# A hybrid decoder step: eight KB of SBUF handed from stage to stage, weights split a step sooner, and a selection step parted in two

## The chip, the cores and the metric

One core of one Trainium2 chip. The metric is the time of one execution on the device, in microseconds. The median of three runs of the kernel before is 2760.28 us (2756.52, 2760.28, 2761.57). The engines: TensorE (PE; its weight loads are written PEld), VectorE (DVE), ScalarE (ACT), GpSimd (POOL), and SyncE (SP), whose queue issues nearly all the DMAs.

## What is computed

One inference step of two layers, for a prompt of 1024 tokens and 8 samples of 8 new tokens each. Layer 0 is attention, layer 1 a recurrent block, and a squared-ReLU MLP follows each. Everything is fp32. The change is all in layer 0 and its hand-over to what follows:

```python
def attn_projections(xn, w_in, a_q_norm, a_k_norm, b_q_norm, b_k_norm):
    h = jnp.einsum('btd,de->bte', xn, w_in)             # one product: 1024 -> 3656 columns
    qa, ka, va, qi, ki, wi, hb = jnp.split(h, list(SPLIT_POINTS), axis=-1)
    q_a = rmsnorm(qa.reshape(bsz, t, A_HEADS, HEAD_DIM), a_q_norm)     # by heads of 64
    ...
    q_b = rmsnorm(hb[:, :, :, 0], b_q_norm[:, None, :])

# prompt, block by block of 128 queries
sc = index_scores(qi_blk, wi_blk, ki)                   # then causal mask
_, idx = lax.top_k(sc, topk)                            # 256 keys of each query
o_a = sparse_attend(q_a, k_a[idx], v_a[idx], ...)       # 8 heads, 2 kv heads
for g, (win, dil) in enumerate(((128, 1), (512, 4), (2048, 16))):
    o, l = dilated_attend(q_b[g], k_b[g], v_b[g], ...)  # local attention, 4 heads
o_b = merge_groups(outs, lses)
y = jnp.einsum('bte,ed->btd', jnp.concatenate([o_a, o_b], axis=-1), w_out)
```

The samples do the same against caches. x + y goes on to the MLP.

## The kernel before

**Stages.** The program is a row of stages, each a block in which every engine has its own list of instructions; between blocks all engines meet at a barrier. In layer 0: `stage_project` (0 to 464 us of PE's time), `stage_window` (local attention, to 574), `stage_sparse` (577 to 729), `stage_sample` (to 776), `stage_out_projection` (from 779). SBUF tensors of a stage are allocated when it is entered, so nothing of the next stage can be loaded before its barrier, except for what `SparseKeys`, `Samples` and `OwnRows` hold.

**fp32 as two halves.** Each fp32 product is three matmul passes: high x high, low x high, high x low. A weight unit of 128 rows is loaded by SP (`load_w`, into `w_raw`, three slots), cast to its high half by DVE (`split_high`, line 881), and its low half, raw minus high, is made by POOL (`split_unit_low`, line 570).

**Projection.** The columns of w_in are taken in eight groups (line 56): kikv (0), qi (1), qa (2), three of qk (3 to 5), v01 (6), v2 (7, half as wide). A group has 9 tiles of up to 128 rows (the first is the 64 sample rows), a tile is 8 units x 3 passes = 24 matmuls into one of three PSUM banks (line 738). PE waits for all eight low halves of a group at its first tile, and for the copy of the tile three before. ACT copies each tile out (line 674), scaled by the row's norm; then for q and k heads the squares (ACT, line 694), sums by head and mean (DVE, lines 912 and 917), root (ACT, line 627), inverse and product (DVE, lines 924 and 928), the gain (POOL, line 596), and the store to DRAM by SP (line 515). The norm is in two parts, `norm_sum` of a tile and `norm_apply` of the one before it. From group 2 on, a step is one (group, tile), and in each of the first eight steps of a group DVE and POOL also split one unit of the next group.

**Selection.** The 256 largest scores of a query are found by bisection on the bits of a bound. For two of the six score tiles DVE itself counts (`Select.count_at`, line 238; a count over 384 and one over 512 scores) and moves the bound (lines 254 and 256: flip, bound), in `Select.step`, once per step. For the four others ACT sums signs (`show`, line 277) and DVE turns their bound (`turn`, lines 288 to 297: count, flip, minus_bound). The main loop of DVE, per step (group, tile):

```python
split_high(gi + 1, i)
if n and STEPS[n - 1] in SHOW_AT: sel.turn(dve, SHOW_AT[STEPS[n - 1]])
norm_sum(gi, i)
norm_apply(*before)
sel.step(dve, y)          # two counts, flip, bound
```

POOL's, per step: `split_unit_low`, then the gains of the tile (two of 256 columns in the qk groups, one of 512 in qa).

**Local attention** runs 24 jobs, each 128 rows of one group: SP loads q, k, v rows (line 1424, 384 KB, eight slots, six ahead) and the bias of each group (line 1429); SP's list begins with row load 0, bias 0, row load 1. PE turns q and k (line 1496), ACT copies them, PE makes scores (1507), DVE adds the bias and finds the maximum (1562), ACT takes the exponent, PE turns the probabilities (1520), PE multiplies by the values (1531), DVE packs (1569), SP stores (1448). PE's list is one job apart per part: turn_rows(t), scores(t-1), turn_probs(t-2), outputs(t-3).

**Sparse attention** begins with turn_keys(0), turn_keys(1) (line 1221), turn_queries(0) (1230), each copied out of the same PSUM bank by ACT (1163), and then scores (1243). SP loads queries of two blocks first (1097).

**Out projection.** SP's list: weight units 0 and 1 (2267), the core's own attention rows a and b (1589, 1596), params, x in four parts (2108, 2111), units 2 and on (2117), two slots. DVE: high half of unit 0, low half of the first mixed rows (`low_of(0)`, line 2341), high half of unit 1, its low half (2358), low_of(1) and on. POOL makes the low half of unit 0 and of units 2 and on (2128). PE: line 2156 for the first two units, 2141 for the others.

## Time and profile before

| | us |
|---|---|
| median of 3 runs | 2760.28 |
| lowest, highest | 2756.52, 2761.57 |
| the profiled execution, its time | 2755.16 |
| its span (first to last instruction) | 2753.3 |
| mean granted TensorE clock, share of full speed | 0.978 |

In layer 0 PE stands still for more than 3 us at eight places:

| PE idle, us | at | before |
|---|---|---|
| 8.93 | 0 | first tile of group 0 |
| 4.56 | 46.8 | group 1 |
| 9.92 | 222.2 | group 3 |
| 6.84 | 463.9 | local attention |
| 3.64 | 573.8 | sparse attention |
| 4.17 | 729.3 | sample stage |
| 12.80 | 776.0 | out projection |
| 3.56 | 811.4 | third weight unit of the out projection |

How to read a row in order of time: start in us from the span's start, duration in us, engine (SPq is the queue of SP), line of the kernel, operation, output<-inputs, how many are taken together, and in brackets the engine's idle time just before with what ended it. PEclk is the granted clock as a share of 2.4 GHz. Matmuls are pipelined, and their ends are modelled; spans on POOL are rough.

### The profile page before, as it was taken

The page shows a single profiled execution, that of the slowest core. Times are in us where ns is not written, and L with a number is a line of the kernel's source. Part 1 is how long each engine was busy: PE and PEld are TensorE (multiplying, and loading weights), DVE is VectorE, ACT ScalarE, POOL GpSimd, SP SyncE. Part 2 cuts the span into 40 slices and gives each one's busy share as a digit, 9 for nine tenths or more (in the row PEclk, how much of TensorE's full clock was granted, in tenths as well). Part 3 has the DMA queues.
Part 4 walks back from the last instruction along what each step waited for, and adds up shares of the span by engine and source line. Part 5 has one row for each costly group of instructions (what it writes and reads, how often), then busy time and mean ns, then how long its engine had stood idle before and what let it go on. Part 6 is the DMA issues. An engine that isn't in the chain of part 4 may idle for free.

```text
span 2753.3 us, 39744 instructions
## 1 busy us (share of the span) xinstructions
PE 2639.0 (96%) x15960; PEld 2450.4 (89%) x15960; DVE 1134.3 (41%) x1978; ACT 779.7 (28%) x1400; POOL 952.7 (35%) x471
## 2 busy tenths in 40 slices
PE   8998998978879999999999999998999999999999
PEld 6666777856659999999999999998999999999999
DVE  5468875335455322222222256655432222222222
ACT  5357773865422110011001033443211001000100
POOL 4214440026335342343334263233344233323422
PEclk8999998989889999999999999999999999999999
DMA  4402223623551111111111112132111111111112
GB/s 147 134 18 83 86 85 104 193 75 109 163 201 47 53 40 46 46 38 46 46 45 39 46 31 86 66 140 111 41 46 47 39 44 46 46 38 46 46 39 87
DMA packets 109196, 198.65 MB, mean 72 GB/s; under 512 B 22709, under 2 KB 62773, under 8 KB 108805
## 3 DMA queue, kind: packets, MB, share of 16 engines
q1 hardware_dynamic: 104602, 191.85, 21.9%
q10 hardware_dynamic: 4480, 5.27, 0.5%
q8 instruction: 72, 1.18, 0.2%
q14 instruction: 42, 0.34, 0.0%
HBM read 170.97 MB, written 47.17 MB: 79 GB/s over the span
## 4 chain that ended last, share of the span: by engine, by line
PE 64%; issue 3%; POOL 2%; DVE 1%; ACT 1%; SPq 1%; DMA 0%; POOLq 0%; DVEq 0%; ACTq 0%
PE d_ps L2141 62%; POOL m_hidden_low L2470 2%; PE d_ps L2763 1%; ACT m_relu L2494 1%; POOL unit_low L2128 1%; DMA unit_raw<-w_units 0%; DVE unit_high L2124 0%; DVE xg_low L2891 0%; SPq L1596 0%; PE d_ps_sums L2199 0%; SPq L1589 0%; DVE r_tanh L2875 0%; SPq L2111 0%; POOLq L2416 0%; DVE r_input_gate L2869 0%
## 5 line engine op out<-in xcount | busy, mean ns | idle before, releaser
L2128 POOL TENSOR_TENSOR unit_low<-unit_raw,unit_high 128x1024 fp32r<-128x1024 f32 x159 | 449.1, 2825 | 1200.8 <-DVE unit_high L2124 1194.8
L2141 PE MATMUL d_ps<-xg_high,unit_high 128*128 128x364 f32 (+1 forms) x2112 | 471.9, 332 | 5.7 <-DVE xg_low L2891 3.1
L2141 PE MATMUL d_ps<-xg_low,unit_high 128*128 128x364 f32 (+1 forms) x2112 | 464.8, 328 | 0.0
L2141 PE MATMUL d_ps<-xg_high,unit_low 128*128 128x364 f32 (+1 forms) x2112 | 464.6, 328 | 0.0
L2494 ACT ACTIVATE m_relu<-d_ps 128x1092 f32<-128x1092 f32 x64 | 69.3, 1083 | 1178.0 <-PE d_ps L2141 1178.0
L2557 DVE TENSOR_TENSOR x_t<-x_t,d_ps 128x1092 f32<-128x1092 f32 x128 | 165.3, 1291 | 520.3 <-PE d_ps L2141 520.3
L2141 PEld LDWEIGHTS d_ps<-xg_high,unit_high 128*128 128x128 f32 x2112 | 365.7, 188 | 11.4 <-DVE xg_low L2891 4.2
L2141 PEld LDWEIGHTS d_ps<-xg_high,unit_low 128*128 128x128 f32 x2112 | 366.6, 188 | 0.0
L2141 PEld LDWEIGHTS d_ps<-xg_low,unit_high 128*128 128x128 f32 x2112 | 365.6, 188 | 0.0
L2141 PE MATMUL d_ps<-m_hidden_high,unit_high 128*128 128x364 f32 (+1 forms) x1536 | 340.7, 330 | 4.0 <-POOL m_hidden_low L2470 4.0
L2141 PE MATMUL d_ps<-m_hidden_high,unit_low 128*128 128x364 f32 (+1 forms) x1536 | 338.5, 328 | 0.0
L2141 PE MATMUL d_ps<-m_hidden_low,unit_high 128*128 128x364 f32 (+1 forms) x1536 | 337.9, 328 | 0.0
L2544 DVE TENSOR_TENSOR m_relu<-m_relu,rstd_all 128x1092 f32<-128x1092 f32 x64 | 86.4, 1350 | 562.3 <-ACT m_relu L2494 562.3
L2141 PEld LDWEIGHTS d_ps<-m_hidden_high,unit_high 128*128 128x128 f32 x1536 | 264.0, 188 | 12.0 <-POOL m_hidden_low L2470 8.8
L2141 PEld LDWEIGHTS d_ps<-m_hidden_high,unit_low 128*128 128x128 f32 x1536 | 266.0, 188 | 0.0
L2141 PEld LDWEIGHTS d_ps<-m_hidden_low,unit_high 128*128 128x128 f32 x1536 | 265.7, 188 | 0.0
L738 PE MATMUL proj_ps<-w_high,x_high 128*128 128x512 f32 (+2 forms) x520 | 202.7, 390 | 16.6 <-POOL w_low L570 16.6
L738 PE MATMUL proj_ps<-w_low,x_high 128*128 128x512 f32 (+2 forms) x520 | 198.9, 382 | 0.0
L738 PE MATMUL proj_ps<-w_high,x_low 128*128 128x512 f32 (+2 forms) x520 | 198.4, 382 | 0.0
L2470 POOL TENSOR_TENSOR m_hidden_low<-m_square,m_hidden_high 128x1092 fp32r<-128x1092 f32 x64 | 164.0, 2562 | 6.4 <-DVE m_square L2549 6.4
L738 PEld LDWEIGHTS proj_ps<-w_high,x_high 128*128 128x128 f32 x520 | 100.0, 192 | 50.0 <-POOL w_low L570 18.6
L2124 DVE CAST unit_high<-unit_raw 128x1024 fp32r<-128x1024 f32 x158 | 112.4, 712 | 59.7 <-PE d_ps L2141 58.7
(354 smaller groups left out, 3084.6 us busy)
## 6 DMA issues: line engine op xcount, KB each, us to landing
unit_raw<-w_units SPq DMA_DIRECT2D x160, 512.0 KB, 3.5
w_raw<-w_in SPq DMA_DIRECT2D x48, 256.0 KB, 2.9
proj_rows<-rows SPq DMA_DIRECT2D x32, 256.0 KB, 2.0
s_win<-win_cache SPq DMA_DIRECT2D x2, 3968.0 KB
sw_rows<-proj_rows SPq DMA_DIRECT2D x16, 384.0 KB, 4.8
proj_rows<-rows SPq DMA_DIRECT2D x36, 128.0 KB, 1.8
select_work<-xt SPq DMA_DIRECT2D x8, 546.0 KB, 3.7
x_t<-xt SPq DMA_DIRECT2D x4, 1092.0 KB, 9.5
```

The costliest lines, as they stand in the source:

```text
L738: last = nc.tensor.matmul(ps[p % 3][:, 0:w], x[:, k, c:c + P], y[gi % 2][:, k, 0:w], start=(n == 0), stop=(n == len(passes) - 1))
L2124: self.nc.vector.tensor_copy(self.wh[slot][:, :], self.raw[:, slot, :]).then_inc(self.w_high, 1)
L2128: self.nc.gpsimd.tensor_tensor(self.wl[slot][:, :], self.raw[:, slot, :], self.wh[slot][:, :].bitcast(F32), ALU.subtract).then_inc(self.w_ ...
L2141: last = self.nc.tensor.matmul(ps[:, c, 0:USED[c]], w[wslot][:, wk], v[:, k, c, 0:USED[c]], start=(k == 0 and n == 0), stop=(k == nk - 1 a ...
L2470: nc.gpsimd.tensor_tensor(hl[:, i, :, :], v[:, i % 2, :, :], hh[:, i, :, :].bitcast(F32), ALU.subtract).then_inc(h_low, 1)
L2494: nc.scalar.activation(r[:, i % 2, :, :], ps[slot][:, :, 0:CH], ACT.Relu).then_inc(d.taken[slot], 1)
L2544: nc.vector.tensor_tensor(r[:, i % 2, :, :], r[:, i % 2, :, :], d.rstd[:, :, :], ALU.mult).then_inc(relu_scaled, 1)
L2557: nc.vector.tensor_tensor(d.x[:, n, :, :], d.x[:, n, :, :], ps[s][:, :, 0:CH], ALU.add).then_inc(d.taken[s], 1)
L2763: last = nc.tensor.matmul(ps[use % 2][:, c, 0:CC], gw[:, n % 2, x, :], cv[:, n % 2, c, :], start=True, stop=True)
```

## The change

1. **A class `Handover`** holds 8 KB of each SBUF partition, allocated from the start of the program to its end, and semaphores that go with it. It is used in turn as the raw weights and gains of the projections, the first two row slots and one turned slot of local attention, the queries of sparse attention, one tensor of new values of the samples, and the raw weight units of the dense stages.
2. **Projection, weights.** Units 0 to 2 of group 3 are loaded, and split by POOL, at the last step of group 1, and cast by DVE among and after the scores; units 3 to 7 go at steps 0 to 4. Of groups 4 and on, each unit is loaded and split one step sooner: unit k at step k - 1 of the group before, and unit 0 at the last step of the group two before (there behind the norms on DVE, behind the gains on POOL).
3. **Projection, DVE's list.** `Select.step` is parted in `try_own` (the two counts), now before `norm_sum`, and `move_own` (flip, bound), after `norm_apply`.
4. **Local attention.** At tile 4 of the last group SP waits for all low halves and for the stores of three tiles, and loads the first two row blocks ahead of the barrier. In the stage bias 0 is loaded first.
5. **Sparse attention.** Both halves of the keys, and the queries of block 0, are turned in the last iterations of local attention (PE, ACT); SP loads two blocks of queries there after store 20. The stage then begins with scores.
6. **Out projection.** Units 0 and 1 and the own rows but those of group 2 are loaded at the end of the sample stage, after waits for the stores of those rows. SP's list in the out projection becomes: own rows of group 2, params, unit 2, x part 0, unit 3, x parts 1 to 3, unit 4 and on. DVE makes both high halves and the second low half, and only then low_of(0).

```diff
+class Handover:
+
+
+    def __init__(self, nc, ctx):
+        self.all = ctx.enter_context(nc.sbuf_tensor("unit_raw", [P, 2, KD * P], F32))
+        self.flat = self.all[:, :, :].rearrange("p u n -> p (u n)")
+        self.rows = self.flat[:, 0:2 * 3 * BW].rearrange("p (s n) -> p s n", s=2)
+        self.rows_in = [ctx.enter_context(nc.semaphore(f"sw_first_in{i}")) for i in range(2)]
+        self.unit_in = [ctx.enter_context(nc.semaphore(f"d_w_in{i}")) for i in range(2)]
...
-        dve.wait_ge(self.done, self.n)
-
-    def step(self, dve, y):
+
+    def try_own(self, dve, y):
+
+        bound = self.bound[:, :].bitcast(F32)
+        self.count_at(dve, range(OWN_TILES), lambda x: bound[:, x:x + 1] if y else 0.0)
+
+    def move_own(self, dve, y):
 
         nc = self.nc
         part = slice(0, OWN_TILES)
-        bound = self.bound[:, :].bitcast(F32)
-        self.count_at(dve, range(OWN_TILES), lambda x: bound[:, x:x + 1] if y else 0.0)
+        dve.wait_ge(self.done, self.n)
         said = self.count[:, part].bitcast(I32)
         if y == 0:
             self.mark(nc.vector.tensor_scalar(self.bound[:, part], said, 31, 1 << 30, ALU.arith_shift_right, ALU.bitwise_xor))
...
-        wraw = sb("w_raw", [P, NRAW, 512])
+        wraw = hand.flat[:, 0:512 * NRAW].rearrange("p (s n) -> p s n", s=NRAW)
...
+        AHEAD_3 = 3
+        WEIGHTS_AT = {n: [] for n in range(len(STEPS))}
+        for k in range(AHEAD_3, KD):
+            WEIGHTS_AT[k - AHEAD_3].append((3, k))
+        for gi in range(4, NGR):
+            for k in range(KD):
+                WEIGHTS_AT[NT * (gi - 3) + k - 1].append((gi, k))
...
-                if gi + 1 < NGR and k < KD:
+                if gi < 2 and k < KD:
                     load_w(gi + 1, k)
+                if gi == 1 and i == NT - 1:
+                    for k in range(AHEAD_3):
+                        load_w(3, k)
+                if gi >= 2:
+                    for unit in WEIGHTS_AT[NT * (gi - 2) + i]:
+                        load_w(*unit)
...
+                if (gi, i) == (NGR - 1, 4):
+                    sp.wait_ge(S["w_low"], KD * NGR)
+                    for n in range(rows_n(gi, 0), rows_n(gi, 3)):
+                        sp.wait_ge(stored[n % NST], stored_total(n))
+                    for t in range(2):
+                        c = TS + P * t
+                        sp.dma_start(hand.rows[:, t, :], proj[c:c + P, 768:768 + 3 * BW]).then_inc(hand.rows_in[t], 16)
...
-                    if gi + 1 < NGR and k < KD:
+                    if gi < 2 and k < KD:
                         split_unit_low(pool, gi + 1, k)
+                    if gi == 1 and i == NT - 1:
+                        for k in range(AHEAD_3):
+                            split_unit_low(pool, 3, k)
+                    if gi >= 2 and i < NT - 1:
+                        for unit in WEIGHTS_AT[NT * (gi - 2) + i]:
+                            split_unit_low(pool, *unit)
                     for h0, hn, row, _ in kinds(gi):
                         n = rows_n(gi, i)
                         pool.wait_ge(S["normed"], NORM_AT[gi, i] + 1)
                         v = st[:, n % NST, HD * h0:HD * (h0 + hn)].rearrange("p (h d) -> p h d", h=hn)
                         nc.gpsimd.tensor_tensor(v, v, gains[:, row:row + 1, :].broadcast_to([P, hn, HD]),
                                                 ALU.mult).then_inc(S["gained"], 1)
+                if gi >= 2:
+                    for unit in WEIGHTS_AT[NT * (gi - 2) + NT - 1]:
+                        split_unit_low(pool, *unit)
                 if gi == 1:
...
+                if j == 6:
+                    split_high(3, 0)
+            for k in range(1, AHEAD_3):
+                split_high(3, k)
...
-            parts = [(sel.step, y) for y in range(BITS + 1)] + [(sel.close, x, z) for x in range(OWN_TILES) for z in range(sel.SLICES)]
+            parts = [("own", y) for y in range(BITS + 1)] + [("close", x, z) for x in range(OWN_TILES) for z in range(sel.SLICES)]
...
-                if gi + 1 < NGR and i < KD:
-                    split_high(gi + 1, i)
+                if i < NT - 1:
+                    for unit in WEIGHTS_AT[n]:
+                        split_high(*unit)
                 if n and STEPS[n - 1] in SHOW_AT:
                     sel.turn(dve, SHOW_AT[STEPS[n - 1]])
+                r1 = min(len(parts), len(parts) * (n + 1) // (last + 1))
+                own = [at[0] for what, *at in parts[r0:r1] if what == "own"]
+                if own:
+                    sel.try_own(dve, own[0])
                 if kinds(gi):
                     norm_sum(gi, i)
                     if before:
@@ -1000,9 +1056,17 @@
                 elif before:
                     norm_apply(*before)
                     before = None
-                r1 = min(len(parts), len(parts) * (n + 1) // (last + 1))
+                if i == NT - 1:
+                    for unit in WEIGHTS_AT[n]:
+                        split_high(*unit)
+                if own:
+                    sel.move_own(dve, own[0])
+                for y in own[1:]:
+                    sel.try_own(dve, y)
+                    sel.move_own(dve, y)
                 for what, *at in parts[r0:r1]:
-                    what(dve, *at)
+                    if what == "close":
+                        sel.close(dve, *at)
...
+    def load_q(self, sp, proj, j):
+        dst = self.q[:, j % 2, :].rearrange("p (r g d) -> p g r d", r=REP, g=AG)
+        for g in range(AG):
+            sp.dma_start(dst[:, g], proj[TS + P * j:TS + P * (j + 1), 256 * g:256 * (g + 1)].rearrange(
+                "p (r d) -> p r d", r=REP)).then_inc(self.q_in[j % 2], 16)
...
-            for n in range(3):
-                take_turn(n)
...
-            turn_keys(0)
-            turn_keys(1)
-            turn_queries(0)
             scores(0)
...
-            load(0)
             load_bias(0)
-            for t in range(1, AHEAD):
+            for t in range(2, AHEAD):
                 load(t)
...
+                if t == NJ - 4:
+                    for j in range(2):
+                        keys.load_q(sp, proj, j)
...
+                if t >= NJ:
+                    take_key_turn(t - NJ, keys.kt[:, 512 * (t - NJ):512 * (t - NJ + 1)])
+            take_key_turn(2, keys.qt[:, 0, :])
...
+            def turn_keys(n):
+                if n == 0:
+                    pe.wait_ge(keys.all_in, 16 * keys.LOADS)
+                    pe.wait_ge(turn_taken, NJ)
+                else:
+                    pe.wait_ge(keys.turn_taken, n)
+                if n == 2:
+                    pe.wait_ge(keys.q_in[0], 16 * AG)
+                for i in range(4):
+                    v = keys.kr[:, 4 * n + i, :] if n < 2 else keys.q[:, 0, P * i:P * (i + 1)]
+                    last = nc.tensor.transpose(psx[:, P * i:P * (i + 1)], v, ident[:, :])
+                last.then_inc(keys.turned, 1)
...
+                if t == NJ + 2:
+                    turn_keys(2)
                 if t >= 3:
                     outputs(t - 3)
+                if NJ <= t < NJ + 2:
+                    turn_keys(t - NJ)
...
+            for x in range(NA):
+                sp.wait_ge(o_out[x % NO], 16 * (x // NO + 1))
+            own.load_a(sp)
+            sp.wait_ge(pv_done, NA + 4)
+            for u in range(2):
+                sp.dma_start(hand.all[:, u, :], a["w_units"][u]).then_inc(hand.unit_in[u], 16)
+            for n, g in enumerate((1, 0)):
+                for x in range(NA + DB // 4 * n, NA + DB // 4 * (n + 1)):
+                    sp.wait_ge(o_out[x % NO], 16 * (x // NO + 1))
+                own.load_b(sp, g)
...
         @block.sync
         def _(sp):
-            for u in range(2):
-                sp.dma_start(d.raw[:, u, :], a["w_units"][u]).then_inc(d.w_in[u], 16)
-            own.load_a(sp)
-            for g in range(NG):
-                own.load_b(sp, g)
-            d.load_first(sp)
-            for u in range(2, KD + 2):
+            own.load_b(sp, 2)
+            d.load_params(sp)
+            for i in range(2):
+                d.load(sp, 2 + i, i)
+                d.load_x(sp, i)
+            for i in range(2, XPARTS):
+                d.load_x(sp, i)
+            for u in range(4, KD + 2):
                 d.load(sp, u, u % 2)
...
             weights_high(0)
-            low_of(0)
             weights_high(1)
             dve.wait_ge(d.w_high, 2)
             nc.vector.tensor_tensor(d.wl[1][:, :], d.raw[:, 1, :], d.wh[1][:, :].bitcast(F32), ALU.subtract).then_inc(second_low, 1)
-            for k in range(1, NK):
+            for k in range(NK):
                 low_of(k)
```

## Rows read from the trace of the kernel before

**Rows 1.** The page, first part: busy time, share of the span, instructions.

```profile
PE 2639.0 (96%) x15960; PEld 2450.4 (89%) x15960; DVE 1134.3 (41%) x1978; ACT 779.7 (28%) x1400; POOL 952.7 (35%) x471
```

**Rows 2.** The waits of PE: us in total, how many times, the longest.

```profile
PE proj_ps L738 <- POOL w_low L570: 16.6, 5, 9.9
...
PE sw_ps_x L1496 <- DMA sw_rows<-proj_rows: 8.6, 2, 6.8
```

**Rows 3.** Busy time by stretches, from four stages; columns in the first row.

```profile
core 0: us, PE busy (x) PEld busy (x) DVE busy (x) ACT busy (x) POOL busy (x), PEclk, DMA share, GB/s
285.96:336.50 50.54, 50.36 (x216) 40.48 (x216) 43.54 (x125) 40.83 (x82) 22.71 (x26) 1.00 0.28 84
438.08:463.93 25.85, 25.85 (x217) 25.65 (x215) 24.80 (x37) 4.50 (x9) 0.00 (x0) 1.00 0.15 49
463.93:483.40 19.47, 9.78 (x56) 7.87 (x57) 3.70 (x18) 7.91 (x24) 0.31 (x1) 0.56 0.67 233
568.70:596.00 27.30, 19.26 (x85) 13.10 (x85) 5.64 (x31) 9.90 (x37) 4.70 (x4) 0.50 0.19 44
```

**Rows 4.** In order of time, around group 3: start, us, engine, line, operation.

```profile
232.15 0.79 PE L738 MATMUL proj_ps<-w_high,x_high 128*128 128x512 f32 x1 [9.92 <-POOL w_low L570]
...
214.59 1.29 POOL L570 TENSOR_TENSOR w_low<-w_raw,w_high 128x512 fp32r<-128x512 f32 x1
...
230.82 1.27 POOL L570 TENSOR_TENSOR w_low<-w_raw,w_high 128x512 fp32r<-128x512 f32 x1
...
232.08 0.67 ACT L674 ACTIVATE rows<-proj_ps,rstd_rows 128x512 f32<-128x512 f32 x1
```

**Rows 5.** In order of time, one step of group 4: DVE, then POOL.

```profile
248.77 0.69 DVE L928 TENSOR_TENSOR rows<-rows,head_inverse 128x512 f32<-128x512 f32 x1
...
251.05 1.22 DVE L256 SCALAR_TENSOR_TENSOR select_bound<-select_flip,select_bound 128x2 int32<-128x2 int32 x1
...
249.54 1.45 POOL L596 TENSOR_TENSOR rows<-rows,gain_rows 128x256 f32<-128x256 f32 x2 [3.15 <-DVE rows L928]
250.94 1.31 POOL L570 TENSOR_TENSOR w_low<-w_raw,w_high 128x512 fp32r<-128x512 f32 x1
```

**Rows 6.** Groups by line, DVE, 286 to 387 us (busy, mean ns).

```profile
L238 DVE TENSOR_SCALAR_CACHE_REDUCE late<-select_work,select_bound 128x384 f32<-128x384 f32 (+1 forms) x34 | 23.0, 676 | 0.6
L256 DVE SCALAR_TENSOR_TENSOR select_bound<-select_flip,select_bound 128x2 int32<-128x2 int32 x17 | 18.5, 1088 | 0.6
...
L912 DVE TENSOR_REDUCE head_sums<-rows_sq 128x8 f32<-128x512 f32 x18 | 12.3, 686 | 11.2 <-ACT rows_sq L694 11.2
...
L297 DVE SCALAR_TENSOR_TENSOR select_minus_bound<-select_flip,select_minus_bound 128x4 int32<-128x4 int32 x13 | 2.1, 163 | 0.4
```

**Rows 7.** In order of time, start of local attention: SP, PE, DVE.

```profile
467.49 0.33 SPq L1424 DMA_DIRECT2D sw_rows<-proj_rows  x1
...
470.77 1.11 PE L1496 MATMUL sw_ps_x<-ident,sw_rows 128*128 128x128 f32 x4 [6.84 <-DMA sw_rows<-proj_rows]
...
476.04 0.29 DVE L1562 CUSTOM_DVE_ANT_0 sw_scores<-sw_ps_s,sw_bias 128x128 f32<-128x128 f32 x1 [10.78 <-PE sw_ps_s L1507]
```

**Rows 8.** In order of time, PE, start of sparse attention.

```profile
577.41 1.09 PE L1221 MATMUL sa_ps_x<-ident,sa_keys 128*128 128x128 f32 x4 [3.64 <-PEq L1369]
...
582.86 1.23 PE L1243 MATMUL sa_ps_s<-sa_keys_t,sa_queries_t 64*128 64x128 f32 x8 [0.69 <-ACT sa_queries_t L1163]
```

**Rows 9.** In order of time, out projection: SP, DVE, PE, DVE, POOL, PE.

```profile
779.04 0.35 SPq L2267 DMA_DIRECT2D unit_raw<-w_units  x1
...
785.73 2.93 DVE L2341 TENSOR_TENSOR mixed_low<-mixed_low,mixed_high 128x1024 fp32r<-128x1024 f32 x1 [0.58 <-ACT mixed_high L2295]
...
788.76 0.94 PE L2156 MATMUL d_ps<-mixed_high,unit_high 128*128 128x364 f32 x2 [12.80 <-DVE mixed_low L2341]
...
810.72 0.69 DVE L2124 CAST unit_high<-unit_raw 128x1024 fp32r<-128x1024 f32 x1 [0.91 <-DMA unit_raw<-w_units]
...
811.49 3.40 POOL L2128 TENSOR_TENSOR unit_low<-unit_raw,unit_high 128x1024 fp32r<-128x1024 f32 x1 [10.40 <-DVE unit_high L2124]
...
814.94 1.27 PE L2141 MATMUL d_ps<-mixed_high,unit_high 128*128 128x364 f32 x3 [3.56 <-POOL unit_low L2128]
```

113 lines of the change are left out of this document (55 added, 58 removed).

## The prediction

> **What bounds the kernel now.** I read four views, in this order. The page: TensorE (PE) is busy for 96% of the span [rows 1], so apart from doing fewer or quicker matmuls, which this change does not attempt, time can only come out of PE's idle stretches and out of stretches where its clock is down. The list of waits, PE first: it names what PE stood still for; the two largest that the change touches are the split weights in the projection stage (16.6 us in five waits, one of 9.9) and the first rows of local attention (8.6 us) [rows 2]. The busy time by stretches: the granted clock is 0.56 after the hand-over from the projections to local attention and 0.50 around the one to sparse attention (1.2 GHz against 2.4 elsewhere) [rows 3], so each hand-over is paid twice, once idle and once slow. Last, the instructions in order of time at each of these places. The dense stages after 830 us wait for little and are not touched.
>
> The profiled execution took 2755.16 us; the median of the runs shown is 2760.28, 5.1 more. I sum against the former and carry the difference over to the median. A measurement of this kernel can tell about 0.2% (5.5 us) from no change.
>
> **Part 1, weights split one step sooner (lines 570, 881).** PE idles 9.92 us before group 3, because the last low half of its weights, unit 7, is made on GpSimd (POOL) at 230.82 and done at 232.09 [rows 4]. With three units split ahead, unit 7 takes the place of unit 4, which POOL began at 214.59 [rows 4], 15 us sooner; PE leaves group 2 at 222.2, so this wait goes whole. The other groups win one step of about 5.6 us, more than any of their waits; of the 16.6 us some 12 can go: the 9.9, and 2 of the other four waits' 6.7, most of which stand before group 1, which is left as it is. The two tiles' worth of slow clock behind the gap can go as well: the first matmul after it takes 0.79 us [rows 4] where the stretch at full clock has 216 in 50.54 us, 5.6 us a tile of 24 [rows 3]; I put this at 2.8 us. If PE alone decided, part 1 would give 12 + 2.8, less a little, **-14.5 us**. The three early casts of VectorE (DVE) lie in waits for the scores, three splits of POOL too; POOL's six mask selects wait behind the latter, but no count reads them before group 2. The loads of SyncE (SP) move with them, one step earlier, and do not pass a store that anyone is late for.
>
> But PE may be only three tiles ahead of the copies by ScalarE (ACT), as it has three banks. ACT copies tile (2,8) at 232.08, 9.9 us after PE made it, since between copies it does the sign passes of the selection (line 277), each of which needs the bound that DVE turned after the last. So once PE waits for no weights, the chain ACT-DVE-POOL decides, and part 2 changes that chain.
>
> **Part 2, DVE's counts ahead of the norms (lines 228 to 256).** Today a step is: cast, turn, head sums, norm, two counts, flip, bound. At 248.77 the norm runs to 249.46; its end releases two gain products on POOL (249.54, 1.45 us together) and the next split (250.94, 1.31) [rows 5]. The counts run beside the gains unhindered. The flip and the bound do not: the bound, two words a lane, takes 1.22 us and ends 0.02 after POOL's split [rows 5]; its mean over 17 is 1088 ns, where the turn's same operation on four words takes 163 [rows 6], mostly while POOL is idle. So DVE and POOL exclude each other for such operations, whoever started first finishing, and one that follows by a semaphore loses to a POOL instruction that is already waiting. The Trainium skill has this as a rule (SBUF — State Buffer, Who interferes with whom): casts, tensor_scalars and anything with two SBUF inputs on VectorE need the port pair shared with GpSimd, for the whole instruction, while a tensor_scalar with an accumulator does not. This trace agrees (1.22 us and unhindered counts), and the rule speaks against the new order.
>
> New order: cast, turn, counts, head sums, norm, flip, bound. Now nothing that is free of the conflict follows the norm. From the norm's end: flip 0.1; bound behind the first gain, 0.85; cast 1.2 and the turn's first operation 1.35; its second behind the second gain, 2.1; its third behind the split, 3.3; then counts 1.45 (two at 676 ns mean and their readouts [rows 6]), head sums to norm 1.7: 6.5 us. A step without a turn: 1.2 + 1.45 + 1.7 = 4.4. Three steps of four have one: mean 6.0 us, against 5.57 to 5.6 of PE. Before, DVE waited 11.2 us in 18 steps for ACT [rows 6], so it needed 5.6 - 0.6 = 5.0. Hence the chain becomes the bound: copies of group 2 come up to 2.5 us later; (3,0) is copied at 236.5 instead of behind PE, (6,0) at 236.5 + 27 x 6.0 = 398.5. There PE may be ahead by between 0 and 9.9 us; I take 4, and then 9 tiles of 5.57 and 9 of 2.87 (nine in 25.85 us [rows 3]), where no gains are left, less the one already made: 398.5 - 4 - 5.6 + 75.9 = 464.8. PE ends this stage at 463.93 now [rows 3]. **Parts 1 and 2 together: +0.9 us.** Bounds: -14.5 where the conflict costs nothing; +9 at 6.3 us a step, if each blocked operation waits 10% longer.
>
> **Part 3, first rows handed over (line 1424).** SP's first instruction of local attention is at 467.49 (row load, 3.3 us to PE's first transpose at 470.77), the first scores are read at 476.04 [rows 7]. With rows 0 and 1 already there, PE starts at 467.5, and two transposes, two copies and the scores need 4.2 us as now: 471.7. The bias, now first in the queue, should need little more than that row load, and lands about then. Saved 4.3; row 2 comes some 0.4 late. **-3.9**, bounds -2 (bias lands last) and -5. SP's wait for three stores at tile (7,4) holds one store back a little, where ACT is busy 4.5 of 25.85 us [rows 3] and can be late; free.
>
> **Part 4, keys and first queries turned before the barrier (lines 1221, 1230).** The first scores of sparse attention start at 582.86; its first transposes began at 577.41 [rows 8]: 5.45 us of turns and copies. They move into the tail of local attention. Two fit into idle spots; the last (turn_keys(2)) waits for ACT's second key copy and stands ahead of the last outputs: up to 2.2 us at the low clock (twice a batch of 1.09 [rows 8]), nothing if it fits in beside them. I take 1.6: **-3.9**, bounds -2.5 and -6. Four query loads on SP stand before the stores of jobs 21 to 23; only the last of these stores holds the barrier, and it has three jobs to make that up. Next to be late is ACT's exponent, as now.
>
> **Part 5, units and own rows loaded in the sample stage (lines 2267, 1589, 1596).** PE waits 12.80 us, to 788.76, for the first low half of the mixed rows: that subtraction took 2.93 us from 785.73 [rows 9] behind POOL's split. The stage starts at 779.0 [rows 9]. With both units there by then the splits run while the mixed rows come in: POOL's done by 782.9, DVE's own low half by 784.1, then the first low half 1.2 us: 785.3, **-3.5**. Unit 2 no longer queues behind the 4.4 MB of x. Its cast, 0.91 us late at 810.72, follows the x addition at once, and POOL's 3.40 us at 811.49 shrink to 2.4 as it starts first [rows 9]: **-1.9** of the 3.56 us idle at 814.94. The matmuls after that gap start slow (three in 1.27 us [rows 9]); I count half of an estimated 1.4 us: **-0.7**. Together -6.1, bounds -2 (mixed rows land no sooner) and -8.5. Own loads sit behind work that is done; the barrier waits for the last stores as before.
>
> **Sum.** +0.9 - 3.9 - 3.9 - 6.1 = **-13.0 us**: 2742.2 for such an execution, **2747.3** as a median.
>
> **Rivals.** (a) *The conflict does not decide*: DVE's short operations slip in ahead of POOL, or ACT's slack swallows them. Then part 1 keeps its gain, -14.5 - 13.9 = -28.4: 2731.9. For it: ACT itself is busy for 40.83 us in nine tiles [rows 3], 4.5 a tile, and could catch up. Against: 17 bounds at 1088 ns [rows 6]. Chance 0.27. (b) *The chain at 6.3 us a step*: +9 - 13.9 = -5, 2755; the same as now. 0.13. (c) *Slower*: each blocked operation waits for two POOL instructions, not one: another 0.9 us a step, 6.9, over 36 steps +33 - 13.9 = +19: 2779. It decides from about 6.5 us a step on (36 x 0.93 = 33 over PE's pace, less the 14.5 of part 1, against 13.9 elsewhere, plus 5.5). Against: every blocked bound ends with one instruction. 0.05. (d) *The hand-overs give half*, since the barriers stay: -6. In the forecast's range. Forecast: 0.55, 2740 to 2754.
>
> The range runs from (a) to (b), 2730 to 2757. Faster by over 0.2% (below 2754.8): the forecast but for a tenth, and (a): 0.79. Slower: (c) and a little: 0.06. Same: 0.15.
>
> **What would show it.** Part 1: no idle before group 3, PE's waits there turn from POOL's w_low to ACT's copies. Part 2: the bound's mean falls below 1 us, but the turn's operations (lines 288 to 297) rise above 0.17 us each, and copies in groups 3 to 5 are 6.0 us apart; at 5.57 rival (a) is right. Part 3: PE's first transpose with SP's first load. Part 4: scores first in the sparse stage. Part 5: PE idle of 9 to 10 us before the out projection. The number fails if the step is not near 6.0, for each 0.1 us is 3 to 4 us.

## The result, and the profile after

The changed kernel takes 2738.06 us (median of 4 runs, 2733.07 to 2744.03) against 2759.95 for the one before: a ratio of 0.9925, 95% interval 0.9908 to 0.9942, so 16 to 25 us are gone. The forecast was 2747.3. The profiled execution took 2744.03 us, its span 2742.2: the longest among its runs, which matters below.

TensorE's landmarks in the two profiled executions (us from the start), and what each stretch between them gained:

| TensorE | before | changed | gained in the stretch | forecast |
|---|---|---|---|---|
| last product of the projections | 463.93 | 465.11 | -1.2 | -0.9 |
| first score of sparse attention | 582.86 | 574.29 | 9.8 | 7.8 |
| last product of sparse attention | 729.29 | 724.13 | -3.4 | 0 |
| last product of the sample stage | 775.96 | 771.46 | -0.7 | 0 |
| first product of the out projection | 788.76 | 783.55 | 0.7 | 3.5 |
| first product of weight unit 2 | 814.94 | 806.75 | 3.0 | 1.9 |
| end of the span | 2753.3 | 2742.2 | 2.9 | 0.7 |

The page of the changed kernel (busy us, share, instructions), the line that answers to [rows 1], and the two longest entries of its list of waits of PE, which answer to [rows 2]:

```profile
PE 2642.6 (96%) x15960; PEld 2452.6 (89%) x15960; DVE 1149.1 (42%) x1978; ACT 781.2 (28%) x1400; POOL 953.9 (35%) x471
```

```profile
PE d_ps L2254 <- DVE mixed_low L2440: 12.1, 1, 12.1
PE proj_ps L785 <- POOL w_low L608: 11.6, 2, 5.9
```

The wait of 9.9 us before group 3 is gone, but the weights still cost 11.6 us in two waits: one before group 1 (5.9, from 47.18 to 53.12) and a new one of 5.65 before group 4. The row of the first product behind it:

```profile
286.17 0.79 PE L785 MATMUL proj_ps<-w_high,x_high 128*128 128x512 f32 x1 [5.65 <-POOL w_low L608]
```

Groups of DVE by line over the same stretch as [rows 6] (L250 is the count, L271 the bound, L303 and L310 the first two operations of the turn; line, operation, count, then busy us and mean ns, then idle before):

```profile
L250 DVE TENSOR_SCALAR_CACHE_REDUCE late<-select_work,select_bound 128x384 f32<-128x384 f32 (+1 forms) x36 | 24.3, 676 | 0.7
...
L271 DVE SCALAR_TENSOR_TENSOR select_bound<-select_flip,select_bound 128x2 int32<-128x2 int32 x17 | 12.1, 712 | 0.6
L310 DVE TENSOR_SCALAR select_flip<-select_count 128x4 int32<-128x4 int32 x14 | 10.8, 768 | 0.5
...
L303 DVE TENSOR_TENSOR select_count<-select_signs,select_level 128x4 f32<-128x4 f32 x14 | 5.4, 387 | 4.0 <-ACT late L292 3.7
```

The bound fell from 1088 to 712 ns, and the turn's operations rose: the second takes 768 ns, the first 387, where (in e1, below) 170 and 235 are to be had. Both are as the list of what to look for said. The third sign of that list, ScalarE's copies 6.0 us apart in groups 3 to 5, or 5.57 if rival (a) is right, came out in between: the nine from (3,0) at 240.51 to (4,0) at 294.72 are 6.02 apart, the 18 from there to (6,0) at 396.33 are 5.65 apart.

One step in order of time, DVE and then POOL (start, us), shows why the turn's operations take longer:

```profile
261.60 0.72 DVE L271 SCALAR_TENSOR_TENSOR select_bound<-select_flip,select_bound 128x2 int32<-128x2 int32 x1
262.24 0.41 DVE L928 CAST w_high<-unit_raw 128x512 fp32r<-128x512 f32 x1
262.95 0.32 DVE L303 TENSOR_TENSOR select_count<-select_signs,select_level 128x4 f32<-128x4 f32 x1 [0.30 <-ACT late L292]
263.31 1.21 DVE L310 TENSOR_SCALAR select_flip<-select_count 128x4 int32<-128x4 int32 x1
...
261.56 1.69 POOL L640 TENSOR_TENSOR rows<-rows,unit_raw 128x256 f32<-128x256 f32 x2 [3.33 <-DVE rows L975]
263.22 1.28 POOL L608 TENSOR_TENSOR w_low<-unit_raw,w_high 128x512 fp32r<-128x512 f32 x1
```

The norm (not shown) releases POOL's two gains at 261.56. The bound, the cast and the turn's first operation squeeze in between and behind them; POOL's split begins at 263.22, and the turn's second operation, begun at 263.31, ends at 264.52, 0.02 after the split (263.22 + 1.28 = 264.50). That is the picture of [rows 5] again, with another victim.

The granted clock by stretches (us, busy us of PE, PEld, DVE, ACT, POOL, then PEclk, DMA share, GB/s), answering to [rows 3]:

```profile
core 0: us, PE busy (x) PEld busy (x) DVE busy (x) ACT busy (x) POOL busy (x), PEclk, DMA share, GB/s
174.00:182.00 8.00, 7.79 (x45) 5.90 (x45) 3.24 (x4) 3.75 (x7) 3.84 (x8) 0.84 0.16 39
182.00:190.00 8.00, 8.00 (x30) 5.61 (x29) 0.89 (x3) 3.39 (x7) 0.24 (x1) 0.50 0.09 29
286.00:387.00 101.00, 100.83 (x423) 81.54 (x424) 93.17 (x253) 81.34 (x162) 48.83 (x53) 0.97 0.29 89
585.00:600.00 15.00, 13.42 (x85) 8.29 (x83) 6.46 (x26) 8.84 (x33) 1.56 (x1) 0.75 0.37 88
```

From 179.4 us, during the small products of the sample scores, the clock stands at 0.50, though TensorE was busy for 7.79 of 8 us; and it was down for two stretches of 3.4 us in sparse attention, where the kernel before had none behind its first scores' slow stretch. Both are in the table above as losses, as the 2.9 us won behind 806.75, where TensorE's list is the same, go with fewer such stretches (one of 3.4 us, against three before; one of those three is the slow start behind 814.94 that the forecast counted at 0.7). Whether they belong to the change is taken up in e0. From 286 to 387 TensorE is busy for 100.83 of 101 us.

Local attention and the first scores of sparse attention, answering to [rows 7] and [rows 8] (PE, DVE, PE):

```profile
468.39 0.63 PE L1578 MATMUL sw_ps_x<-ident,unit_raw 128*128 128x128 f32 x4 [3.29 <-PEq L371]
...
472.41 0.29 DVE L1648 CUSTOM_DVE_ANT_0 sw_scores<-sw_ps_s,sw_bias 128x128 f32<-128x128 f32 x1 [5.97 <-DMA sw_bias<-window_strips]
...
574.29 1.23 PE L1298 MATMUL sa_ps_s<-sa_keys_t,unit_raw 64*128 64x128 f32 x8 [3.64 <-PEq L1421]
```

And the out projection, answering to [rows 9] (SP's load of two weight units, an ACT copy that waits for a store, the first instruction of the stage on POOL, the first product, the first product of unit 2):

```profile
766.21 0.83 SPq L1858 DMA_DIRECT2D unit_raw<-w_units  x2
...
774.13 0.38 ACT L1950 ACTIVATE ss_merged_t<-ss_ps_x 128x256 f32<-128x256 f32 x1 [4.18 <-DMA mixed_t<-ss_merged_t]
...
777.64 0.15 POOL L2376 MEMSET ones_square<- 128x64 f32 x1 [7.71 <-POOLq L1771]
...
783.55 0.94 PE L2254 MATMUL d_ps<-mixed_high,unit_high 128*128 128x364 f32 x2 [12.10 <-DVE mixed_low L2440]
...
806.75 0.76 PE L2239 MATMUL d_ps<-mixed_high,unit_high 128*128 128x364 f32 x3 [1.53 <-POOL unit_low L2226]
```

### The profile page after: what moved, and what is told of

Its sections match the earlier page's. It is cut to its first block, busy times and chain, and to the rows that moved or that the text cites. A ratio compares the mean times of both kernels' runs of the same rounds, so it can differ in the third digit from the quotient of the medians.

```text
span 2742.2 us, 39751 instructions
## 1 busy us (share of the span) xinstructions
PE 2642.6 (96%) x15960; PEld 2452.6 (89%) x15960; DVE 1149.1 (42%) x1978; ACT 781.2 (28%) x1400; POOL 953.9 (35%) x471
## 4 chain that ended last, share of the span: by engine, by line
PE 64%; issue 3%; POOL 2%; DVE 1%; ACT 1%; POOLq 0%; DVEq 0%; ACTq 0%
PE d_ps L2239 63%; POOL m_hidden_low L2568 2%; PE d_ps L2861 1%; ACT m_relu L2592 1%; PE d_ps L2254 1%; POOL unit_low L2226 1%; DVE unit_high L2222 0%; DVE xg_low L2989 0%; PE d_ps_sums L2297 0%; DVE unit_low L2456 0%; DVE r_tanh L2973 0%; POOLq L2514 0%; DVE r_input_gate L2967 0%; DVE r_tanh L2961 0%; DVE x_t L2655 0%
## 5 line engine op out<-in xcount | busy, mean ns | idle before, releaser
L2239 PEld LDWEIGHTS d_ps<-m_hidden_low,unit_high 128*128 128x128 f32 x1536 | 265.7, 188 | 0.0
L785 PE MATMUL proj_ps<-w_high,x_high 128*128 128x512 f32 (+2 forms) x520 | 203.1, 391 | 11.7 <-POOL w_low L608 11.6
L785 PEld LDWEIGHTS proj_ps<-w_high,x_high 128*128 128x128 f32 x520 | 100.3, 193 | 44.1 <-POOL w_low L608 12.3
```

Source lines behind the costliest of these rows:

```text
L785: last = nc.tensor.matmul(ps[p % 3][:, 0:w], x[:, k, c:c + P], y[gi % 2][:, k, 0:w], start=(n == 0), stop=(n == len(passes) - 1))
L2239: last = self.nc.tensor.matmul(ps[:, c, 0:USED[c]], w[wslot][:, wk], v[:, k, c, 0:USED[c]], start=(k == 0 and n == 0), stop=(k == nk - 1 a ...
```

## Experiments

Each kernel is the changed one with the edit shown. "Ratio" is to the kernel before, run in the same session. Where stretches of the profile are compared, a half-clock stretch is named if it is in one and not in the other.

### e0: the changed kernel again

> The changed kernel once more, as it is, to see which of its stretches repeat. The profile after shows the clock at half from 179.4 to 193.1 us and from 592.4 and 636.8 us, at places where the kernel before had it whole. Theory A: these are chance of one execution; then a second profile has its half-clock stretches elsewhere, PE ends the projections some 5 to 7 us sooner (458 to 460 instead of 465.1), and the span is near 2732 to 2736. Theory B: they come with the change (the weight splits moved in front of the sample scores); then they stand at the same places again and PE ends the projections at 465 again. In both the median is 0.991 to 0.994 of the kernel before.

Measured: 2737.25 us, ratio 0.9925 (0.9909 to 0.9942). Its profiled execution has nearly the same slow stretches (13.7 us from 178.4, 3.4 from 591.4 and from 635.8) and the same wait of 5.67 us before group 4; the projections end at 464.42. By this run alone theory B (they come with the change) stood. The later runs with the very same projection code took that away: executions of f1, f2 and g1 have no half-clock stretch at 179 and end the projections at 459.52, 459.52 and 458.99, that of g2 has it and ends at 463.99. The same two rows, of the kernel f2 (keys back, projection unchanged):

```profile
174.00:182.00 8.00, 7.81 (x61) 6.23 (x60) 3.24 (x4) 3.49 (x8) 4.08 (x8) 1.00 0.26 65
182.00:190.00 8.00, 8.00 (x37) 5.95 (x36) 6.00 (x20) 2.80 (x5) 0.00 (x0) 1.00 0.01 4
```

So of six executions of this projection three had the slow stretch, and they end the stage 4.5 to 6.1 us later. The stretch itself costs 4.1 to 4.7 of that: from the start of GpSimd's 21st split to that of its 28th (162.97 to 199.41 in the changed kernel) it takes 36.1 to 36.7 us with it and 32.0 without; the rest was there before. In the four executions with the counts behind the norms (the kernel before, e1, e3, h1) the stretch did not occur; that is too few to say whether it is chance. The two short ones in sparse attention come and go likewise: with none of them that stage takes 146.4 to 146.6 us (before, e1, f1, h1), with one 147.8 (e2, h3), with two 149.7 to 149.8 (the changed kernel, e0, e3, g1); in f2, g2 and h2 the slow stretch at the stage's start was itself longer. The 3.4 us that the table shows as given back are these. What decides whether an execution has them was not found; up to 179 us the six kernels ran the same instructions.

### e1: counts behind the norms again (part 2 undone)

```diff
-                if own:
-                    sel.try_own(dve, own[0])
                 if kinds(gi):
...
                 if own:
+                    sel.try_own(dve, own[0])
                     sel.move_own(dve, own[0])
```

> The changed kernel with part 2 alone undone: the two counts stand again behind norm_apply, right before flip and bound; weights stay a step sooner, hand-overs stay. Theory (the port that VectorE and GpSimd share decides): the counts behind the norm cover the gains, VectorE's step falls from 5.74 us (turn steps 6.26, others 4.2) to below TensorE's 5.57, the 5.65 us wait for the weights of group 4 is gone, and TensorE ends the projections 8 to 14 us sooner than in the changed kernel, at 451 to 457; the bound's mean goes back to about 1.1 us. Ratio to the kernel before some 0.987 to 0.990. Rival (the order is not what decides; the wait at group 4 comes from the late start of the steps): TensorE's end moves by less than 2 us. Second rival (the new order was worth something, since ScalarE's root gets its sums at once): it ends later than 467.

Measured: 2732.37 us, ratio 0.9910 (0.9892 to 0.9927). The first product of group 4, and the same groups of DVE over the same stretch:

```profile
275.62 0.51 PE L785 MATMUL proj_ps<-w_high,x_high 128*128 128x512 f32 x1 [2.25 <-POOL w_low L608]
...
L271 DVE SCALAR_TENSOR_TENSOR select_bound<-select_flip,select_bound 128x2 int32<-128x2 int32 x16 | 16.2, 1014 | 0.5
...
L303 DVE TENSOR_TENSOR select_count<-select_signs,select_level 128x4 f32<-128x4 f32 x14 | 3.3, 235 | 2.9 <-ACT late L292 2.8
...
L310 DVE TENSOR_SCALAR select_flip<-select_count 128x4 int32<-128x4 int32 x14 | 2.4, 170 | 0.5
```

The projections end at 453.43, without a slow stretch at 179; against the 459.0 to 459.5 of the executions of the changed projection that had none either, the new order costs 5.6 to 6.1 us. Counted from GpSimd's 28th split, behind the slow stretch, it is 5.7 to 6.2: 265.2 to 265.7 us to the end of the stage in the six executions of the changed projection, 259.5 in e1 and in h1, which has the same order as e1. Both are below the 8 to 14 expected, since nearly half of the distance to 465.11 was the clock. The wait before group 4 is 2.25 instead of 5.65, not gone. The turn's operations are back at 235 and 170 ns, the bound at 1014. The rivals (no change, or later than 467) are out. By times the two kernels are 4.9 us apart, and the intervals of the ratios overlap, though each of the five runs of e1 (2728.73 to 2735.81) is shorter than each of the five of e0 (2736.23 to 2746.56).

### e2: weights at the old steps (part 1 undone)

```diff
-        AHEAD_3 = 3
+        AHEAD_3 = 0
...
-                WEIGHTS_AT[NT * (gi - 3) + k - 1].append((gi, k))
+                WEIGHTS_AT[NT * (gi - 3) + k].append((gi, k))
...
-                if j == 6:
-                    split_high(3, 0)
-            for k in range(1, AHEAD_3):
-                split_high(3, k)
```

> The changed kernel with part 1 alone undone: every weight unit is loaded and split at the step of the kernel before, counts stay ahead of the norms. Theory (shared port): now the slower chain of VectorE also makes the weights late; a wait of about 10 us before group 3 is back, there are more before groups 4 to 6, and TensorE ends the projections at 475 to 480, 10 to 15 us later than in the changed kernel. Ratio to the kernel before about 1.000. Rival (the order costs nothing): only the 9.9 us and the slow clock behind it come back and the end is at 464 plus 1 to 5, that of the kernel before plus little.

Measured: 2756.09 us, ratio 0.9990 (0.9978 to 1.0002); the projections end at 481.14 (with the slow stretch at 179). All that the hand-overs win is lost again. Its waits of PE for weights:

```profile
PE proj_ps L785 <- POOL w_low L608: 24.7, 5, 11.6
```

One before each of the groups 1 and 3 to 6 (11.64, 2.89, 1.80 and 2.45 us for the latter). In e3, with the same weight steps and the old order, they are 16.8 us in five waits: with weights just in time, the slower steps of DVE go into them.

### e3: both at once (hand-overs alone)

The two edits above together.

> The changed kernel with parts 1 and 2 undone, so the hand-overs between stages alone are left (parts 3, 4 and 5). TensorE ends the projections at 464 as in the kernel before (within 1.5 us); what is won comes behind it. Theory (my sum for these parts): 13.9 us, 0.995 of the kernel before. Rival (half of it is given back behind the gaps, as the profile after hints for sparse attention, where 3.4 us of 8.6 are lost again by 724 us): 7 to 10 us, 0.9965.

Measured: 2744.68 us, ratio 0.9947 (0.9928 to 0.9966); the projections end at 464.64, as before. The hand-overs are worth 14.9 us by medians, where the forecast's sum for them was 13.9. The four kernels make a square, medians in us:

| | counts behind the norms | counts ahead |
|---|---|---|
| weights at the old steps | 2744.7 | 2756.1 |
| weights one step sooner | 2732.4 | 2737.3 |

Part 1 alone is worth 12.3, part 2 alone costs 11.4; on top of part 1 it costs 4.9. TensorE's waits for weights show the same: the new order adds 7.9 us to them at the old weight steps (16.8 to 24.7) and 2.9 with weights a step sooner (8.7 to 11.6), where the weights' lead swallows the rest.

### h2: GpSimd's gains made small

```diff
-                        v = st[:, n % NST, HD * h0:HD * (h0 + hn)].rearrange("p (h d) -> p h d", h=hn)
-                        nc.gpsimd.tensor_tensor(v, v, gains[:, row:row + 1, :].broadcast_to([P, hn, HD]),
+                        v = st[:, n % NST, HD * h0:HD * (h0 + hn)].rearrange("p (h d) -> p h d", h=hn)[:, :, 0:1]
+                        nc.gpsimd.tensor_tensor(v, v, gains[:, row:row + 1, 0:1].broadcast_to([P, hn, 1]),
```

> The changed kernel, with the gain products of GpSimd cut to one column in 64 of each head (so 63 of 64 columns of queries and keys go without their gain); their number and all waits stay. It takes 1.3 to 1.45 us of GpSimd's work out of each step. Theory (VectorE's short operations behind the norm wait for GpSimd's gains and split): the turn's first and second operations fall from 460 and 776 ns to below 250, VectorE's step falls below TensorE's 5.57, and TensorE ends the projections at 446 to 454 (459.5 in executions of the changed projection without the half-clock stretch at 179 us, 465 with it). Rival (it is the order itself, ScalarE being asked for its root and squares later): 458 or later.

Measured: 2727.51 us, ratio 0.9884 (0.9865 to 0.9904); the projections end at 449.05, no wait before group 4. The bound and the turn's second operation:

```profile
L271 DVE SCALAR_TENSOR_TENSOR select_bound<-select_flip,select_bound 128x2 int32<-128x2 int32 x15 | 2.6, 172 | 0.5
...
L310 DVE TENSOR_SCALAR select_flip<-select_count 128x4 int32<-128x4 int32 x13 | 2.2, 170 | 0.4
```

Not an instruction of DVE was touched, and the bound went from 712 to 172 ns, the turn's second operation from 768 to 170. So what held them was GpSimd's work, not the order of ScalarE's requests. The order matters by what it leaves under that work.

### h3: flip and bound ahead of the norm as well

```diff
                 if own:
                     sel.try_own(dve, own[0])
+                    sel.move_own(dve, own[0])
...
-                if own:
-                    sel.move_own(dve, own[0])
```

> The changed kernel with flip and bound moved too: counts, flip, bound, then head sums and norm; so no operation of the own bound stands behind the norm, but neither do the counts. Theory (what costs is that nothing free of the conflict follows the norm and covers the gains; cast and turn now wait for them): no gain, TensorE ends the projections at 458 to 462 (or 464 to 467 with a half-clock stretch at 179 us), turn's operations still above 400 ns, the bound's mean below 200. Rival (what costs is flip and bound alone, being first in line behind the gains): the end comes at 452 to 455.

Measured: 2740.27 us, ratio 0.9937 (0.9915 to 0.9960); the projections end at 464.10, without a slow stretch at 179: 4.6 us or more later than in the changed kernel, worse than either expectation. Waits of PE for weights (us, times, longest), and two groups of DVE:

```profile
PE proj_ps L785 <- POOL w_low L608: 15.3, 3, 7.0
...
L310 DVE TENSOR_SCALAR select_flip<-select_count 128x4 int32<-128x4 int32 x13 | 11.2, 862 | 0.4
...
L303 DVE TENSOR_TENSOR select_count<-select_signs,select_level 128x4 f32<-128x4 f32 x13 | 6.8, 523 | 4.8 <-ACT late L292 4.8
```

The bound is quick now (224 ns), but the turn's three operations rose to 523, 862 and 481 ns (from 387, 768 and 312) and the flip to 367 (from 226). By the sums of these groups the bound saves 8.5 us and the others give back 5.8, so these sums alone do not explain the later end; the steps do: from norm to norm a step with a turn takes 6.5 us instead of 6.3, one without 4.8 instead of 4.2, and TensorE waits 6.99 us before group 4 and 2.33 before group 5. Taking one victim away from behind the norm moved the others forward into the gains.

### f1: rows loaded in the stage again (part 3 undone)

```diff
-                if (gi, i) == (NGR - 1, 4):
-                    sp.wait_ge(S["w_low"], KD * NGR)
...
-                        sp.dma_start(hand.rows[:, t, :], proj[c:c + P, 768:768 + 3 * BW]).then_inc(hand.rows_in[t], 16)
...
+            load(0)
             load_bias(0)
-            for t in range(2, AHEAD):
+            for t in range(1, AHEAD):
```

> The changed kernel with part 3 alone undone: no row is loaded ahead of the barrier; local attention's queue begins with row 0, bias 0, row 1 again. In the kernel before TensorE's last product of the projections and its last of local attention are 109.85 us apart (463.93 to 573.78), in the changed one 105.54 (465.11 to 570.65), with the turned keys inside. Theory: part 3 is worth 4 us, so they are 109 to 110 apart here. Rival (bias 0 comes last, and the row loaded ahead wins only the first transpose): 106.5 to 107.5. By times alone the step (0.15%) is too small to be told.

Measured: 2739.42 us, ratio 0.9934 (0.9918 to 0.9951). The first scores are read 11.83 us after TensorE's last product of the projections, against 7.30 and 7.62 in the two executions of the changed kernel (and 12.11 before): 4.2 to 4.5 us. The whole stage took 107.73 us, where the expectation named 109 to 110 for 4 us and 106.5 to 107.5 for less. That comparison was badly chosen: the 105.54 it was set against holds a half-clock stretch of 6.8 us in mid-stage (537.8) that this run lacks, as do seven others (e1, e2, e3, g2, h1, h2, h3), which took 101.5 to 103.4. Against these it is 4.3 to 6.2. Part of that is the clock behind the hand-over: in f1 it stands at half for 17.1 us from 464.7, as in the kernel before (17.1 from 466.3), and for 6.8 to 13.7 us in all executions that load the rows ahead.

### f2: keys turned in sparse attention again (part 4 undone)

The turns and their copies go back to the stage's start, the query loads too:

```diff
-                if t == NJ + 2:
-                    turn_keys(2)
...
-                if NJ <= t < NJ + 2:
-                    turn_keys(t - NJ)
...
+            turn_keys(0)
+            turn_keys(1)
+            turn_queries(0)
             scores(0)
```

> The changed kernel with part 4 alone undone: keys and first queries are turned at the start of sparse attention again, and loaded there. From TensorE's last product of the projections to its first score of sparse attention it is 118.9 us in the kernel before and 109.2 in the changed one. Theory (part 4 is worth 5.45 less what the turns cost in the tail): 113 to 114.5 here, and local attention itself (105.54 in the changed kernel) gets 0 to 2 us shorter. Rival (the turns lengthen the tail by nearly what they save): it gets 3 us or more shorter, and the first score comes at most 2 us later than in the changed kernel.

Measured: 2742.57 us, ratio 0.9944 (0.9927 to 0.9961). Between local attention's last product and the first score lie 9.08 us, as before, against 3.64: 5.44 us. Local attention took 102.29 us, in the middle of those seven with the turns inside (101.5 to 103.4), so the rival is out. The tail shows why nothing is to be seen. The first turn of probabilities after the last scores, and the last outputs, first in the changed kernel, then in f2:

```profile
564.14 0.66 PE L1602 MATMUL sw_ps_t<-ident,sw_scores 128*128 128x128 f32 x4 [0.85 <-ACT sw_scores L1544]
...
569.65 1.00 PE L1613 MATMUL sw_ps_o<-sw_rows,sw_probs_t 128*128 128x64 f32 x8
```

```profile
555.37 0.66 PE L1615 MATMUL sw_ps_t<-ident,sw_scores 128*128 128x128 f32 x4 [0.85 <-ACT sw_scores L1560]
...
559.86 1.94 PE L1626 MATMUL sw_ps_o<-sw_rows,sw_probs_t 128*128 128x64 f32 x8 [0.61 <-DVE sw_out_rows L1664]
```

The turned keys put the last outputs 1.0 us later (5.51 us behind that turn instead of 4.49), but these then run at full clock, in 1.00 us instead of 1.94: in f2 the granted clock fell to half at 559.5, ahead of them, in the changed kernel at 571.9, after the last product. All eleven executions with the turns inside have these 1.00 us and fell later. From the projections' end to the first score it is 111.36, below the 113 expected, for the same reason as above.

### g1, g2: weight units, or own rows, behind the barrier (part 5 in halves)

```diff
-            for u in range(2):
-                sp.dma_start(hand.all[:, u, :], a["w_units"][u]).then_inc(hand.unit_in[u], 16)
...
+            for u in range(2):
+                sp.dma_start(d.raw[:, u, :], a["w_units"][u]).then_inc(d.w_in[u], 16)
             own.load_b(sp, 2)
```

> The changed kernel, but weight units 0 and 1 are loaded behind the barrier of the out projection again; the own rows stay ahead of it. In the changed kernel the out projection starts 6.2 us after TensorE's last product of the sample stage (771.46, 777.64), in the one before 3.1 (775.96, 779.03). Theory A (the megabyte of weights issued at 766.2 fills the DMA engines, so that the last stores land in over 4 us instead of 1.9, and ScalarE waits 4.2 us for one of them): here the stage starts 3 to 3.5 us after that product, but the units then arrive late, and the first product of the out projection is some 12.5 to 13.5 us after it, as before. Theory B (SyncE's eight small loads of own rows, 574 ns each and slower ones behind waits, hold the barrier): the start stays at 5.5 us or more.

Measured: 2739.70 us, ratio 0.9931 (0.9914 to 0.9948). The last product of the sample stage ends at 765.50. The landing of the stores to mixed_t (count, KB, median us from issue to landing) and the start of the stage:

```profile
mixed_t<-ss_merged_t ACTq DMA_DIRECT2D x4, 128.0 KB, 2.2
...
769.12 0.15 POOL L2376 MEMSET ones_square<- 128x64 f32 x1 [5.15 <-POOLq L1771]
```

The same line of the changed kernel, over its last 5 us of the sample stage and the barrier:

```profile
mixed_t<-ss_merged_t ACTq DMA_DIRECT2D x4, 128.0 KB, 5.3
```

The stage starts 3.62 us after the last product instead of 6.19, and the stores land in 2.2 us instead of 5.3: theory A. The first product comes after 15.10 us, even later than the 12.5 to 13.5 expected. Two rows of DVE say why:

```profile
777.00 1.10 DVE L2436 CAST unit_high<-unit_raw 128x1024 fp32r<-128x1024 f32 x1 [1.87 <-DMA unit_raw<-w_units]
...
779.28 6.90 DVE L2440 TENSOR_TENSOR mixed_low<-mixed_low,mixed_high 128x1024 fp32r<-128x1024 f32 x6
```

The high half of the first mixed rows is ready 6.6 us after the stage's start, when the kernel before began their low half (6.7 us after). But DVE's new list has the cast and the low half of unit 1 first, and that unit lands only at 776.98, so the low half begins 10.2 us after the start. The new list pays only with the units there.

The other half keeps the units ahead and puts the small loads back:

```diff
-                own.load_b(sp, g)
...
-            own.load_b(sp, 2)
+            for g in range(NG):
+                own.load_b(sp, g)
```

> The changed kernel, but the window rows of the own samples (12 small loads) are loaded behind the barrier of the out projection again; the weight units and the sparse rows stay ahead of it. Theory A (the megabyte of weights delays the last stores): the stage still starts 5 us or more after TensorE's last product of the sample stage. Theory B (the small loads hold the barrier): it starts 3 to 3.5 us after it, and, with both units there, the first product of the out projection comes 9 to 9.5 us after that last product instead of 12.1.

Measured: 2740.64 us, ratio 0.9933 (0.9916 to 0.9950). The stage starts 5.82 us after the last product, the first product comes after 11.79. Of the 3.1 us by which the start had moved, the small loads hold 0.4, the units 2.6.

### h1: units earlier, counts back: a faster version

On the kernel with the counts behind the norms:

```diff
+            sp.wait_ge(pv_done, NA)
+            load_new(0)
+            for u in range(2):
+                sp.dma_start(hand.all[:, u, :], a["w_units"][u]).then_inc(hand.unit_in[u], 16)
             sp.wait_ge(pv_done, NA + 2)
             load_new(2)
...
             sp.wait_ge(pv_done, NA + 4)
-            for u in range(2):
-                sp.dma_start(hand.all[:, u, :], a["w_units"][u]).then_inc(hand.unit_in[u], 16)
```

> The kernel with the counts back behind the norms, and the weight units 0 and 1 loaded earlier in the sample stage: when the first four items are done (some 14 us before the stage's end, a second into which no last store falls) instead of 5 us before its end. To free the handed 8 KB for that, the new values of one group go elsewhere (the place of the sparse items' values, which is then free, and of own rows not loaded yet). Theory (the units' megabyte delays the last stores of the sample stage when it is issued among them): the out projection starts 3 to 3.8 us after TensorE's last product of the stage instead of 6.1, its first product 9 to 10 us after it instead of 12.1 to 12.3; the whole is 2 to 3 us faster than with the counts back alone, near 0.990 of the kernel before. Rival (the barrier is late because of something else on SyncE): start at 5.5 or more, no gain. Second rival (the loads now delay something within the sample stage): that stage takes 44 us or more instead of 42.5 to 43.2.

Measured: 2728.97 us, ratio 0.9897 (0.9878 to 0.9916). Start of the stage, and its first product:

```profile
755.38 0.15 POOL L2387 MEMSET ones_square<- 128x64 f32 x1 [5.11 <-POOLq L1770]
...
761.39 0.94 PE L2265 MATMUL d_ps<-mixed_high,unit_high 128*128 128x364 f32 x2 [9.59 <-DVE mixed_low L2451]
```

With the last product of the sample stage at 751.80, these are 3.58 and 9.59 us, and the sample stage itself took 42.97, as in most others (42.5 to 43.2). The first product comes 2.5 to 2.75 us sooner than with the units among the last stores. The step from 2732.37 is within the intervals, so that it is a gain of time rests on the rows. That this version beats the kernel before rests on the times themselves; by the ratios of two sessions (0.9897 and 0.9925) it is some 8 us below the changed kernel.

## Why the prediction was right, and where not

**Sum and sign.** -13.0 us forecast, about -21 measured (0.9925 of 2760); the range to 2730 held it, but 2738.06 lies below the 2740 to 2754 given the largest chance, about midway between the forecast and rival (a). The profiled execution even had the very 2742.2 us of span that I summed for its time, and ended the projections at 465.11 where 464.8 was forecast. Both are chance: it was the slowest of four, with over 4 us of slow clock at 179 that the sum did not have. Against the square of medians, parts 3 to 5 were forecast at -13.9 and are -14.9; parts 1 and 2 were forecast at +0.9 and are -7.4. Nearly the whole error is there. (The chance of "faster" was added up wrongly: 0.55 less a tenth and 0.27 make 0.77, not 0.79.)

**Part 1.** -14.5 if TensorE alone decides; -12.3 alone, by medians. Right in mechanism. The 9.9 us wait went, as said. What was missed is group 4: even with the counts back 2.25 us of wait stand there. From e3 to e1 the waits for weights fall by 8.1 us (16.8 to 8.7), not 12; besides group 4, 1.7 us of the difference is a longer wait before group 1, which h1, with the same projection code as e1, does not have. The sign given, that TensorE's waits turn from w_low to ScalarE's copies, failed: waits for copies are 0.8 us at most in the six executions.

**Part 2.** The conflict, its victims and its direction were right. The size was not: the failed term is the 6.0 us step in groups 4 and 5. f2, whose projection is the changed one and has no slow stretch, can be set against the sum term by term. (3,0) is copied at 234.98 (forecast 236.5). The nine steps to (4,0) are 6.02 us apart, as forecast; the 18 to (6,0) are 5.65, so that (6,0) is copied at 390.82, not 398.5. From there to TensorE's end it takes 68.7 us, forecast 66.3: its lead is 1.6 us, not 4. Together 459.5 instead of 464.8. The steps of VectorE were a little too long in the sum too: 6.26 us with a turn, not 6.5, and 4.2 without, not 4.4, a mean of 5.74. But above all the slower chain is charged once, not up to group 6: in all six executions TensorE waits 5.65 to 5.70 us before group 4, and from there to the end of the stage it takes 178.5 to 179.0 us, within 1 us of the kernel before (285.96 to 463.93 [rows 3]). Group 4's weights come late because POOL's splits follow DVE's steps; behind it TensorE never waits for a copy, so a step 0.17 over its 5.57 is covered by its lead (f1 and g2 wait another 0.6 to 0.7 us for weights before group 5). The rule of the Trainium skill that was weighed there (SBUF — State Buffer, Who interferes with whom: one port pair for both engines, locked for a whole instruction) holds: with GpSimd's gains cut, VectorE's bound takes 172 ns.

**Rival (a)**, that the conflict does not decide, is half true: the conflict decides for some 6 us (4.9 by medians), not for the 15 between (a) and the forecast. (b) and (c) needed 6.3 us a step and more; no run of the changed kernel came near, but with the old weight steps the same order costs 11.4.

**Part 3.** -3.9 forecast, -4.2 to -4.5 at the first scores. The bound "bias lands last" (-2 instead of -3.9) came true as a fact, since DVE's first instruction waits for sw_bias (472.41), but costs little: the first scores are read 1.60 us after TensorE starts them, against 1.39 in the kernel before and 1.39 to 2.24 in the other versions with rows loaded ahead. The sum had no term for the clock, which stands at half for 10.3 us behind this hand-over instead of 17.1.

**Part 4.** -3.9 forecast, -5.4 measured. The failed term is the 1.6 us for turn_keys(2) ahead of the last outputs. It delays them by 1.0 us, and it was sized at the low clock; with the turns inside the clock stays up to the end of the stage, and the outputs give 0.94 us of it back.

**Part 5.** -3.5 for the first product, -0.7 measured. The idle time before unit 2 fell from 3.56 to 1.53 us, -2.0 for the forecast -1.9; the rest of the 3.0 that the stretch between the two products gained is the clock, which is back at full 3.5 us after the first product instead of 5.2. The slow start behind unit 2 (0.7 in the sum) is gone. The sign given, 9 to 10 us of idle time before the stage's first product, failed (12.1) and came only with h1 (9.59). The failed step is the sentence "the barrier waits for the last stores as before". It waits for them, but not as before: a megabyte of weights is issued at 766.21, just ahead of them, and the next three stores (issued at 767.71, 769.01 and 770.69) land in 6.3, 5.7 and 4.8 us, against 2.9, 1.9 and 1.9 in g1 and 3.2, 2.6 and 1.9 in the kernel before. The DMA engines' share from 766.2 to 775 is 0.75, against 0.52 in g1; g1 shows the cause, the queueing itself is inferred. The barrier comes 3.1 us later, which eats the 3.8 won behind it.
